# Steps of a mixer that runs between gather slots are moved one to five slots later

## The chip, the cores and the metric

The kernel runs on one core of a Trainium2 chip. The metric is the time of one launch in microseconds (us) on the device; the median of three runs is compared. A difference of under 0.2% (5 us) is not told from none here.

## What is computed

Two layers of a transformer-like backbone over 256 latent tokens `x` and 256 context tokens `ctx`, width 1024, float32. Cut to what matters:

```
for l in range(2):
    z = split(modulate(rms_norm(x), ...) @ w_in[l])          # 1968 columns, three mixers side by side
    mix = concat(pool_mixer(z), attention(z), mlstm(z)) @ w_out[l]
    x = x + g_a * mix                                        # context likewise, except in the last layer
    h = modulate(rms_norm(x), ...)
    q = (h @ peer_wq[l]); s = q . subkeys                    # 8 heads, two halves, 128 keys each
    experts = top 16 of the pair sums, per head              # 128 experts per token
    a = gelu(h . u_tab[expert]);  w = softmax(best) * a
    x = x + g_f * sum(w * v_tab[expert])
```

Each of the 128 tokens of a tile asks for 128 experts, each a row of 1024 `u` and 1024 `v` values (8 KB).

## The kernel before

**Slots.** The expert part runs over slots. In slot m, GpSimd (POOL) issues one gather of a row for each of 128 partitions, 1 MB together, into a free place (L772). VectorE (DVE) multiplies it with the token rows (`dot`, L1544). ScalarE (ACT) turns the sum into a coefficient and a diagonal matrix (`gated`, L1080, L1081, L1084: `gact`, `coef`, `diag`). TensorE (PE) adds the weighted `v` half (`values`, L1964); up to slot 336 of layer 0 it does two slots at a time, in the odd one. Then the place is free, and the next gather into it may be issued. Layer 0 has 512 slots (two context tiles, then two x tiles), layer 1 has 256.

**What runs between.** Mixer p stands for a layer and stream: p = 0 is the context's mixer of layer 0, before all slots and alone; p = 1, x's of layer 0, runs between slots 0 to about 200; p = 2, keys and values of the context in layer 1, from slot 268; p = 3 runs alone before layer 1's slots. Every engine's program is a generator that yields the slot number at which its next piece stands. `merge` puts the pieces in order, and `Behind.run(m)` gives out what is due after the engine's own work of slot m. So each engine has one fixed order, written out ahead; nothing is moved at run time, and a piece that waits holds up that engine's later slots.

**Places.** In slots 0 to 71 there are 7 places for gathered rows, then 8, from 134 on 9, and from 180 on more.

**Steps of p = 1 that the change touches** (slot of each in brackets):
- `norm1`: eight squares on ACT (L792; two each in 0 to 3), summed by PE (L1647; 2 to 5), `mean` on DVE (L1217; 6), `root` on ACT (L796; 7), `inverse` on DVE (L1221; 8), scaling on DVE and `modulate` on ACT.
- `projected`: ACT copies each of 16 groups of the input projection out of PSUM, three slots after PE begins it (L848 to L866).
- `gates`: ACT takes a logarithm (16, L873 to L875), DVE begins with it (17, L1252), PE turns the result (25), ACT copies it (26).
- `low_rank`: squares, `mean`, `root` and `inverse` of two further norms.
- the mLSTM, four heads, `ml` = 63, `ml_step` = 7. For head h, after 63 + 7h: PE makes scores (0, 1), DVE masks them (1, `masked`, L1334), ACT takes exponentials (2, `memory`, L928 and L931), DVE multiplies (4, 5, `weighted`, L1346), PE makes numerators (6, 7, L1764), ACT copies these (8, `numbers`, L939). `masked` of the next head waits for this head's numerators.

**Queries** for the experts are made between slots as well. PE forms query n in slots up to `ASKED[n]` (L1922), ACT copies it (`asked`, L1046), PE scores the keys two slots on (L1932), ACT copies these (`keys`, L1057, L1061), and DVE picks the best (L1472). One buffer `b_query` holds a query's sum: the next query's first part waits for `asked`. The weights of a query come into a ring of two (`qring`), loaded by SyncE (SP) once the scores of the query two before are done.

**SP** issues all weight loads in the one order of `ORDER`. `later` is four loads: the second part of `con`, layer 1's `par`, x itself and `poolw` (L748 to L751).

## Time and profile before

| what | value |
|---|---|
| median of three runs | 2608.3 us (2607.79 to 2610.45) |
| the profiled run | 2614.96 us |
| span of its trace | 2613.1 us |
| busy: PE, DVE, ACT, POOL | 2113.3, 1671.7, 1131.2, 819.3 us |
| moved by DMA | 940.07 MB, 805.36 MB of it by gathers |
| first gather issued, last row of PE's values in layer 1 begun | about 251 us, about 2601 us |

In a profile an instruction's own time is given beside the idle time of its engine before it, and behind an arrow what ended that idle time. Idle time alone costs nothing; it counts where the thing that is short (here mostly the DMA engines' time) is not used because of it.

### The profile page before, as it was taken

The numbers are of one execution on the slowest core, as the hardware profiler recorded it, in microseconds if no ns is written. First come the engines' busy times: TensorE is split into PE (matmuls) and PEld (weight loads), VectorE is DVE, ScalarE is ACT, GpSimd is POOL, SyncE is SP. The second block draws the span as 40 slices with busy tenths as digits, with TensorE's granted clock in tenths as the row PEclk, the third lists the DMA queues.
The fourth block names the chain that finished last, engine by engine and source line by source line (L and its number), as shares of the span: only waits on it lengthen the run. The fifth ranks groups of instructions, "written<-read, shape, count | busy, mean of one in ns | idle before, by whom it ended". The sixth has DMA issues, their size and how long they took to land.

```text
span 2613.1 us, 26759 instructions
## 1 busy us (share of the span) xinstructions
PE 2113.3 (81%) x8372; PEld 994.3 (38%) x8372; DVE 1671.7 (64%) x4135; ACT 1131.2 (43%) x3279; POOL 819.3 (31%) x772
## 2 busy tenths in 40 slices
PE   7988899776887777885777777699989987777776
PEld 4658555332443333441121111176874321211111
DVE  3484657678886766767667775335446666677654
ACT  3352544556663434644343333245333343433333
POOL 0000323343444334434434333100014443343331
PEclk8989999788999889997999999988899999999999
DMA  9783899999999999999999999811129999999997
GB/s 369 309 339 159 310 359 419 371 368 420 419 389 420 419 410 420 412 419 420 421 420 421 421 421 421 353 51 49 55 116 420 420 420 421 421 420 421 421 421 303
DMA packets 135885, 940.07 MB, mean 360 GB/s; under 512 B 14912, under 2 KB 18368, under 8 KB 25664
## 3 DMA queue, kind: packets, MB, share of 16 engines
q0 software_dynamic: 110592, 805.36, 75.0%
q1 hardware_dynamic: 23968, 131.70, 12.9%
q8 instruction: 66, 1.08, 0.2%
q10 hardware_dynamic: 1184, 1.32, 0.2%
q14 instruction: 75, 0.61, 0.1%
HBM read 937.27 MB, written 1.05 MB: 359 GB/s over the span
## 4 chain that ended last, share of the span: by engine, by line
DMA 45%; PE 36%; DVE 9%; ACT 7%; issue 2%; POOL 1%; SPq 1%; DVEq 0%; POOLq 0%; ACTq 0%
DMA mix<-uv_dram,idx 22%; DMA fast<-uv_dram,idx 19%; PE bank L1964 12%; PE bank L1922 5%; PE bank L1675 4%; DMA qring<-wq_dram 3%; DVE fast L1544 3%; PE bank L1880 2%; PE bank L1932 1%; PE bank L1669 1%; PE bank L1764 1%; DMA fast<-w_dram 1%; DVE mix L1544 1%; ACT diag L1084 1%; ACT coef L1081 1%
## 5 line engine op out<-in xcount | busy, mean ns | idle before, releaser
L1964 PE MATMUL bank<-fast,diag 128*64 128x512 f32 x2064 | 821.8, 658 | 257.4 <-ACT diag L1084 253.9
L772 POOL DMA_INDIRECT fast<-uv_dram,idx x516 | 559.8, 1085 | 1348.5 <-PE bank L1964 721.8
L1544 DVE SCALAR_TENSOR_TENSOR fast<-fast,hrow 128x1024 f32<-128x1024 f32 x516 | 630.4, 1223 | 358.9 <-DMA fast<-uv_dram,idx 354.0
L1080 ACT ACTIVATE gact<-araw 128x1 f32<-128x1 f32 x768 | 153.9, 200 | 855.2 <-DVE fast L1544 559.0
L1964 PEld LDWEIGHTS bank<-fast,diag 128*64 128x64 f32 x2064 | 198.2, 144 | 731.3 <-ACT diag L1084 469.9
L1964 PE MATMUL bank<-mix,diag 128*64 128x512 f32 x748 | 350.4, 622 | 100.2 <-ACT diag L1084 100.2
L1544 DVE SCALAR_TENSOR_TENSOR mix<-mix,hrow 128x1024 f32<-128x1024 f32 x187 | 229.0, 1226 | 151.7 <-DMA mix<-uv_dram,idx 151.6
L772 POOL DMA_INDIRECT mix<-uv_dram,idx x187 | 189.9, 1016 | 290.7 <-PE bank L1964 260.0
L1084 ACT ACTIVATE diag<-con,coef 128x64 f32<-128x64 f32 x768 | 267.1, 348 | 25.3
L1081 ACT ACTIVATE coef<-gact,wts 128x1 f32<-128x1 f32 x768 | 226.1, 294 | 25.0
L1964 PEld LDWEIGHTS bank<-mix,diag 128*64 128x64 f32 x748 | 84.6, 138 | 328.2 <-ACT diag L1084 219.4
L1922 PE MATMUL bank<-hT,qring 128*128 128x256 f32 x576 | 175.2, 420 | 34.1 <-DMA qring<-wq_dram 24.0
L1922 PEld LDWEIGHTS bank<-hT,qring 128*128 128x128 f32 x576 | 102.2, 197 | 140.8 <-issue 101.3
L1964 PE MATMUL bank<-hT,diag 128*64 128x512 f32 x204 | 101.8, 623 | 25.4 <-ACT diag L1084 25.3
L1544 DVE SCALAR_TENSOR_TENSOR hT<-hT,hrow 128x1024 f32<-128x1024 f32 x51 | 62.6, 1227 | 38.8 <-DMA hT<-uv_dram,idx 34.3
L1675 PE MATMUL bank<-hT,back 128*128 128x256 f32 (+1 forms) x336 | 83.7, 388 | 4.0 <-ACT hT L821 4.0
L1046 ACT ACTIVATE pq<-bank 128x256 f32<-128x256 f32 (+1 forms) x56 | 19.6, 350 | 134.7 <-PE bank L1922 134.5
L772 POOL DMA_INDIRECT hT<-uv_dram,idx x51 | 54.1, 1060 | 75.5 <-PE bank L1964 66.8
L1675 PE MATMUL bank<-hT,fast 128*128 128x256 f32 (+1 forms) x320 | 74.7, 389 | 1.3 <-ACT hT L821 1.3
L1675 PEld LDWEIGHTS bank<-hT,back 128*128 128x128 f32 (+1 forms) x336 | 63.8, 190 | 15.1 <-issue 4.4
L1080 ACT ACT_TABLE_LOAD x53 | 68.0, 1283 | 1.0
L1675 PEld LDWEIGHTS bank<-hT,fast 128*128 128x128 f32 (+1 forms) x320 | 60.2, 192 | 13.9 <-issue 5.4
(270 smaller groups left out, 2604.4 us busy)
## 6 DMA issues: line engine op xcount, KB each, us to landing
fast<-w_dram SPq DMA_DIRECT2D x72, 1024.0 KB, 8.3
qring<-wq_dram SPq DMA_DIRECT2D x36, 576.0 KB, 8.3
back<-w_dram SPq DMA_DIRECT2D x20, 1024.0 KB, 9.5
fast<-uv_dram,idx POOLq DMA_INDIRECT x516, 19.9
mix<-wq_dram SPq DMA_DIRECT2D x12, 576.0 KB, 10.4
mix<-uv_dram,idx POOLq DMA_INDIRECT x187, 23.9
fast<-uq_dram SPq DMA_DIRECT2D x4, 576.0 KB, 4.8
back<-uq_dram SPq DMA_DIRECT2D x2, 576.0 KB, 7.7
```

The costliest lines, as they stand in the source:

```text
L772: g.indirect_dma_start(slot(e, m), None, uv_tabs[e], bass.IndirectOffsetOnAxis(idx[:, Q % 2, n:n + 1], 0)).then_inc(landed[place], 16)
L1080: link(a.activation(gact[:, n:n + 1], araw[:, Q % 2, n:n + 1], ACT.Gelu))
L1081: link(a.activation(coef[:, n:n + 1], gact[:, n:n + 1], ACT.Copy, scale=wts[:, Q % 2, n:n + 1]))
L1084: a.activation(diag[:, m % DIAGS, :], two, ACT.Copy, scale=coef[:, n:n + 1]).then_inc(diag_ready.sem, 1)
L1544: v.scalar_tensor_tensor(out=u, in0=u, scalar=1.0, in1=hrow[:, (2 * i + half) % 3, :], op0=ALU.mult, op1=ALU.mult, accum_out=araw[:, Q % 2 ...
L1669: mm = t_.matmul(bank[g % 2][:, 0:WT], own_h(p)[:, k, n * P:(n + 1) * P], w[:, k, :], start=(k == 0), stop=(k == KC - 1))
L1675: mm = t_.matmul(bank[g % 2][0:rows, 0:SEQ], w[:, k, o:o + rows], own_h(p)[:, k, :], start=(k == 0), stop=(k == KC - 1))
L1764: mm = t_.matmul(memory_banks(p)[3][:, o:o + MD + 1], mE[:, e, kc, q * P:(q + 1) * P], v1[:, kc % 2, h, :], start=(kc == kcs[0]), stop=(kc ...
L1880: mm = t_.matmul(bank[b % 2][:, cs], w[:, k, b % 2 * P:b % 2 * P + P], own_h(p)[:, k, cs], start=(k == 0), stop=(k == KC - 1))
L1922: mm = t_.matmul(dst[:, cs], query_tile(e, u)[:, k, :], own_h(p)[:, k, cs], start=(k == 0), stop=(k == KC - 1))
L1932: mm = t_.matmul(b_aside[rows, j * P:(j + 1) * P], pq[:, n % 2, j * HALF:(j + 1) * HALF], query_tile(e, u)[:, KC, :], start=True, stop=True)
L1964: mm = t_.matmul(acc[half, f * 512:(f + 1) * 512], diag[:, j % DIAGS, :], slot(e, j)[:, D + f * 512:D + (f + 1) * 512], start=(j % SLOTS < ...
```

## The change

For p = 1, all but the attention, steps that wait for another engine are put one to five slots later (`lag`, and spelled out in `norm1`, which holds for p = 2 too). `asked` stands one slot later and `keys` two, in both layers. SP's `later` stands three weight loads later. No instruction is added or taken out. The core of the diff:

```diff
+def lag(p, slots_):
+    return slots_ if p == 1 else 0
...
-    order.append((-2000 + ADA_FIRST + 0.5, "later", 0))
+    order.append((-2000 + ADA_FIRST + 3.5, "later", 0))
...  # ACT, norm1
-                    yield k // 2 - early(p)
+                    yield k // 2 * (1 if alone(p) else 2) - early(p)
-                yield 7 - early(p)
+                yield 7 - early(p) + 2 * (not alone(p))
                 root(p, 1)
-                    yield 9 + (k + 1) // 3
+                    yield 9 + (k + 1) // 3 + (not alone(p))
...  # ACT, projected
-                    yield in_at(g) + 3
+                    yield in_at(g) + 3 + lag(p, 1)
...  # ACT, gates
-                yield GATE_AT + 3
+                yield GATE_AT + 3 + lag(p, 2)
-                    yield GATE_AT + 8
+                    yield GATE_AT + 8 + lag(p, 3)
-                yield GATE_AT + 11
+                yield GATE_AT + 11 + lag(p, 5)
...  # ACT, low_rank
-                yield at + 5
+                yield at + 5 + lag(p, 1)
-                            yield at + 3
+                            yield at + 3 + lag(p, 2)
-                    yield at + 7
+                    yield at + 7 + lag(p, 2)
...  # ACT, memory, then numbers
-                    yield at + 2
+                    yield at + 2 + lag(p, 1)
-                    yield TIMES[p].ml + TIMES[p].ml_step * h + TIMES[p].num + 2
+                    yield TIMES[p].ml + TIMES[p].ml_step * h + TIMES[p].num + 2 + lag(p, 2)
...  # ACT, experts
-                    if m in answer:
-                        asked(e, answer[m])
-                    if m - 2 in answer:
-                        keys(e, answer[m - 2])
+                    if m - 1 in answer:
+                        asked(e, answer[m - 1])
+                    if m - 4 in answer:
+                        keys(e, answer[m - 4])
...  # DVE, norm1 (mean, inverse, scaling)
-                yield 6 - early(p)
+                yield 6 - early(p) + 3 * (not alone(p))
-                yield 8 - early(p)
+                yield 8 - early(p) + 2 * (not alone(p))
-                    yield 8 + (k + 1) // 3 - early(p)
+                    yield 8 + (k + 1) // 3 - early(p) + 2 * (not alone(p))
...  # DVE, gates
-                at = GATE_AT + 2
+                at = GATE_AT + 2 + lag(p, 3)
...  # DVE, low_rank: mean and inverse, twice
-                yield at + 4
+                yield at + 4 + lag(p, 2)
-                yield at + 6
+                yield at + 6 + lag(p, 2)
-                    yield at + 6
+                    yield at + 6 + lag(p, 3)
-                    yield at + 8
+                    yield at + 8 + lag(p, 4)
...  # DVE, masked, weighted, combine
-                    yield TIMES[p].ml + TIMES[p].ml_step * h + 1
+                    yield TIMES[p].ml + TIMES[p].ml_step * h + 1 + lag(p, 2)
-                        yield TIMES[p].ml + TIMES[p].ml_step * h + 4 + e
+                        yield TIMES[p].ml + TIMES[p].ml_step * h + 4 + e + lag(p, 1)
-                yield at
+                yield at + lag(p, 2)
-                yield at + 1
+                yield at + 1 + lag(p, 1)
...  # PE, norm1, then gate_turns
-                    yield k // 2 + 2 - early(p)
+                    yield (k // 2 + 2 if alone(p) else k // 2 * 2 + 1) - early(p)
-                yield GATE_AT + 10
+                yield GATE_AT + 10 + lag(p, 3)
```

## Rows read from the trace of the kernel before

**Rows 1.** The page: busy times, and GB/s in 40 equal slices of the span.
```profile
PE 2113.3 (81%) x8372; PEld 994.3 (38%) x8372; DVE 1671.7 (64%) x4135; ACT 1131.2 (43%) x3279; POOL 819.3 (31%) x772
...
GB/s 369 309 339 159 310 359 419 371 368 420 419 389 420 419 410 420 412 419 420 421 420 421 421 421 421 353 51 49 55 116 420 420 420 421 421 420 421 421 421 303
```

**Rows 2.** Busy times by stretch: PE, PEld, DVE, ACT, POOL, then PEclk, DMA share, GB/s.
```profile
280.00:390.00 110.00, 98.73 (x458) 61.40 (x459) 68.50 (x168) 56.73 (x160) 34.94 (x32) 0.94 0.90 337
390.00:460.00 70.00, 64.38 (x287) 40.17 (x287) 51.48 (x128) 29.85 (x91) 23.53 (x23) 0.98 1.01 419
460.00:570.00 110.00, 83.72 (x353) 41.56 (x354) 75.07 (x186) 65.61 (x173) 45.01 (x38) 0.81 0.91 360
570.00:720.00 150.00, 111.61 (x504) 49.23 (x500) 133.16 (x351) 100.41 (x250) 66.81 (x57) 0.90 1.01 420
720.00:770.00 50.00, 40.08 (x206) 20.05 (x206) 38.95 (x104) 34.79 (x88) 22.45 (x19) 0.97 0.97 379
...
960.00:1060.00 100.00, 79.18 (x360) 35.86 (x360) 65.63 (x172) 42.99 (x145) 44.73 (x37) 0.91 1.00 410
```

**Rows 3.** Waits from 280 to 390 us: in total, times, longest.
```profile
ACT pq L1046 <- PE bank L1922: 16.9, 6, 4.8
...
DVE rms L1217 <- PE bank L1647: 12.9, 2, 6.7
PE bank L1964 <- ACT diag L1084: 12.7, 5, 4.4
...
DVE mix L1252 <- ACT mix L875: 8.8, 1, 8.8
```

**Rows 4.** Timeline of PE at slot 27: start, length, idle before.
```profile
372.48 0.70 PE L1922 MATMUL bank<-hT,qring 128*128 128x256 f32 x2 [1.69 <-DMA qring<-wq_dram]
```

**Rows 5.** The chain that ended last, at the same place: start, length.
```profile
361.31 11.13 DMA qring<-wq_dram
```

**Rows 6.** Waits from 460 to 570 us.
```profile
PE bank L1964 <- ACT diag L1084: 26.3, 6, 6.4
...
ACT mix L939 <- PE bank L1764: 10.7, 4, 4.4
DVE mix L1334 <- PE bank L1764: 10.3, 3, 4.8
```

**Rows 7.** Timeline of all engines around slots 71 to 73.
```profile
507.87 0.39 ACT L939 ACTIVATE mix<-bank 128x260 f32<-128x260 f32 x1 [4.38 <-PE bank L1764]
507.94 1.41 DVE L1334 TENSOR_TENSOR mix<-con,bank 128x256 f32<-128x256 f32 x4 [4.79 <-PE bank L1764]
509.27 1.22 DVE L1544 SCALAR_TENSOR_TENSOR qring<-qring,hrow 128x1024 f32<-128x1024 f32 x1
...
511.02 1.27 DVE L1544 SCALAR_TENSOR_TENSOR fast<-fast,hrow 128x1024 f32<-128x1024 f32 x1
511.46 1.28 ACT L928 ACT_TABLE_LOAD   x1
...
517.22 0.20 ACT L1080 ACTIVATE gact<-araw 128x1 f32<-128x1 f32 x1
518.18 1.11 PE L1964 MATMUL bank<-qring,diag 128*64 128x512 f32 x1 [6.36 <-ACT diag L1084]
```

**Rows 8.** Timeline of PE: the values of two slots, without and with idle time before.
```profile
489.42 1.94 PE L1964 MATMUL bank<-fast,diag 128*64 128x512 f32 x8
495.39 3.68 PE L1964 MATMUL bank<-fast,diag 128*64 128x512 f32 x8 [4.04 <-ACT diag L1084]
```

**Rows 9.** Timeline of PE in mixer 0, first expert-free stage.
```profile
39.85 1.94 PE L1610 MATMUL bank<-fast,hT 128*32 128x256 f32 x16 [4.68 <-DMA fast<-w_dram]
...
49.52 2.86 PE L1675 MATMUL bank<-hT,fast 128*128 128x256 f32 x12
```

**Rows 10.** Timeline of SP's queue: start, length of the issue.
```profile
18.13 0.43 SPq L748 DMA_DIRECT2D con<-con_dram  x1
...
19.81 10.72 SPq L751 DMA_DIRECT2D poolw<-pw_dram  x1
```

**Rows 11.** DMA issues: KB each, us to landing.
```profile
xT<-x_dram SPq DMA_DIRECT2D x1, 1024.0 KB, 18.1
...
con<-con_dram SPq DMA_DIRECT2D x1, 713.0 KB, 14.3
```

## The prediction

> **What bounds the kernel now.** I read the page first. The figure to see is GB/s in slices: 420 or 421 in most of both expert stages [rows 1]. There the DMA engines are full, and a slot costs what its megabyte costs: 1.05 MB / 421 GB/s = 2.49 us. Work of PE, DVE or ACT in such a slice is hidden by the queued gathers. The PE's 81% is an average that misleads: it says nothing of these slices.
>
> So I went by stretches and asked of each how much DMA time is unused, length x (1 - GB/s / 421) [rows 2]. From 280 to 390 us (slots 1 to 34): 110 x (1 - 337/421) = 21.9 us. From 460 to 570 us (slots 57 to 93, the mLSTM): 110 x (1 - 360/421) = 15.9 us. From 720 to 770 us (attention): 5.0 us. From 960 to 1060 us (where mixer 2 begins): 2.6 us. 390 to 460 and 570 to 720 us together: under 1 us. That is about 45 us, the most that any reordering between slots could give. Whatever the change does elsewhere is covered, as long as the places stay full.
>
> Then the waits of the two large stretches. In the first, PE is busy 98.7 of 110 us [rows 2]: PE itself is nearly the bound, so only its idle time can be won, 11.3 us. 12.7 us stand against `diag`, of which 4.4 are before slot 0 is valued [rows 3], not reached by the change: 8.3 us are. The engines behind those: DVE waits 12.9 us for the sums of squares and 8.8 us for the logarithm, ACT 16.9 us for queries [rows 3]. Each wait takes away the lead of DVE or ACT over PE, and PE pays when it comes to the next values. In the second, PE is idle 26.3 us of 110 and waits for `diag` in all of it [rows 2, 6].
>
> **Startup: `later` moves behind three weight loads.** PE waits 4.68 us for a weight tile, until 39.85 us [rows 9]. Ahead of that tile in SP's order stand `later`'s loads from 18.13 us on, and SP is held 10.72 us on their last [rows 10]. They are 1024 + 713 KB [rows 11] and, by the code, 261 KB of `par` and 64 KB of `poolw`: 2.1 MB, 5.0 us at 421 GB/s. So the tile lands near 34.8 us, about when PE began to wait (35.2). But the fourth tile after it still has the same bytes ahead of it: 39.8 + 3 x 2.49 = 47.3 us. It is the first that PE needs in its next projection group, at 49.52 us before [rows 9]. PE would be there at 44.8 and waits for it to 47.3. So of 4.68 us 2.5 come back as a wait, and 2.2 us are won; mixer 0 is then PE's own time. Bounds: 0 and 4.7. What is late next: x lands 7.5 us later, near 45 us, just before DVE's gates need it. I take -2.2.
>
> **Slots 0 to 34.** Squares go to every second slot, DVE's mean from slot 6 to 9, the gates from 17 to 20, the mean of the second norm from 25 to 27; each then stands behind the PE or ACT step it waits for, by one to four slots. The 12.9 and 8.8 us of DVE waits should go nearly whole, and DVE's dots run on. ACT's queries wait a slot less. Of the 8.3 us of PE idle I take 6: from slot 16 to 27 there is a second bound, the ring of query weights. Its load is issued when PE has scored the query two before, takes 11.13 us [rows 5], and PE already waits 1.69 us for it [rows 4]; three slots have to pass in that time, so a faster PE waits longer there. New costs: the gates' result comes three slots later, and nothing reads it before slot 50; ACT's pool copy and DVE's first use of it now stand in one slot (34), about 1 us on DVE, in a stretch with full DMA. Bounds: +6 (rival 3's query parts at half) and -11.3 (all PE idle). I take -6.
>
> **The mLSTM, slots 63 to 95.** One head in detail [rows 7]: DVE waits 4.79 us for the numerators of head 0, masks in 1.41 us, dots slot 72 at once and slot 73 at 511.02. ACT, also held by the numerators, makes `diag` of slot 72, then its burst of exponentials from 511.46 to 517.22 (5.8 us, two table loads in it), and only then `diag` 73. PE waits 6.36 us. The holds stand one behind the other: wait, mask, burst. After the change mask, burst and copy stand in slot 73. DVE and ACT do slots 72 and 73 first, in the time in which they waited, since those rows had landed: neither dot has idle time before it. PE then has two more slots of values ready, 1.94 us a pair when nothing idled before [rows 8], and the wait for numerators is over or short. The burst stays. Before: (10.3 + 10.7) us of waits for numerators in all [rows 6]; they overlap, so 10.3 once. Four heads: 26.3 us of idle less 10.3 less 4 x 1.94 = 8 us remain. New prices: ACT waits for the mask in its own slot, up to 1.4 us a head, 5.6 us on ACT; in slot 95 ACT waits for DVE's combine, about 2 us. In slot 87 the last head's exponentials follow the gates' softmax at once, which spares ACT one pair of table loads, 2 x 1.28 = 2.6 us [rows 7]. All that is PE idle time; the DMA time unused is 15.9 us and can't be won twice. With 18 of 26 us of the cause gone, less 5.6 for the mask, I take half and a bit: -9. Bounds: +6 (the mask's price alone) and -15.9.
>
> On the table loads the Trainium skill ("ScalarE: Activation LUTs", What ACT_TABLE_LOAD costs) puts a drain of about 1.38 us beside the 1.28 us, so the pair spared would be an estimated 5.3 us. The trace has no room for it: of the burst's 5.76 us two loads take 2.56, which leaves 0.40 us for each of its eight exponentials, and two drains more would leave 0.06; I go by 1.28.
>
> **The rest.** `asked` and `keys` later: from slot 203 on and in layer 1 DMA is full and places are many; `keys` stays ahead of the choice that reads it by two slots (slot 30 for 32, 62 for 64, 222 for 224). Mixer 2's norm: 2.6 us unused there; -0.5. Attention: untouched, 0. These are costed at nothing because of the gathers queued; were those stages not full, each `asked` would lay a query part (1.1 us) behind `diag` on PE.
>
> **Sum.** -2.2 - 6 - 9 - 0.5 = -17.7 us. The profiled run is 2614.96 us (span 2613.1), 6.7 over the median; the differences I take to be the same in both, so 2608.3 - 17.7 = 2590.6, say 2591.
>
> **Rivals.**
> 1. *Another engine's wait takes over* (DVE in the mLSTM, the query ring in slots 16 to 27). DVE is busy 75 of 110 us there [rows 2]; with the burst of 5.8 us still standing, each head may still miss the DMA by what it did less the wait. Then only a third is won: -2.2 - 2 - 4 = -8, 2600.
> 2. *All of it, and the clock.* After idle time the same eight matmuls take 3.68 us instead of 1.94 [rows 8], and from 460 to 570 us the granted clock is 0.81 [rows 2], so PE is at its lower level (1.2 of 2.4 GHz) some 38% of the time. If the idle gaps close, PE also gets faster, and the mLSTM stretch fills the DMA: -4 - 9 - 15.9 = -29, 2579. The Trainium skill ("TensorE: Matmul & The Clock Gate", HAM oscillation) prices such idling at half of the throttled time, here an estimated 21 us of PE time; by it this rival would be the forecast.
> 3. *No lead to spend* (slower). The later steps help only if DVE and ACT can pass PE by two slots, which needs landed rows. With 7 or 8 places, a row lands only after PE frees its place; if the rows aren't there, every wait stays and the prices come on top: 5.6 for masks, 2 for combine, and for queries 8 to 15 a part of 1.1 to 2.05 us laid behind `diag` on PE, 12.5 us in all. At half of that, with startup's 2.2 gone as well: +10, 2618. It decides where a dot after a stall has idle time for a landing. Against it: the dots of slots 72 and 73 had none [rows 7].
> 4. *Nothing measurable*: gains of slots 0 to 34 eaten by the query ring, the mLSTM's by the burst: 2606.
>
> **How the numbers follow.** Forecast (-12 to -23) 0.48; rival 1 0.20; rival 2 0.13; rival 4 0.11; rival 3 0.08. The predicted time is the forecast's. Faster by over 0.2% is the forecast and rivals 1 and 2, 0.81; within 0.2% 0.11; slower 0.08. The range leaves out rival 3 and the outer parts of 2 and 4: 2576 to 2607. The forecast's own range is 2585 to 2596.
>
> **What would show it.** Right: GB/s of the fifth and sixth slice (261 to 392 us) up from 310 and 359, of the eighth and ninth from 371 and 368 towards 420; DVE's waits at L1217 and L1252 of p = 1 under 2 us; PE's first rest tile near 35 us without idle time, and a new wait of some 2.5 us at the next group; granted clock in the mLSTM over 0.85; first gather issued about 2 us sooner. Wrong: ACT idle before L928 of over 2 us a head (the masks' price), dots waiting for DMA landings before slot 95, or longer waits for `qring`.

## The result, and the profile after

The changed kernel takes 2593.7 us (2587.5 to 2597.9 in six runs; a seventh was disturbed and doesn't count) beside 2610.45 us (2606.1 to 2615.3 in seven) for the kernel before. The ratio is 0.9929, with a 95% interval from 0.9915 to 0.9943: 0.0071 x 2610 = 18.5 us less (the two medians alone lie 16.8 us apart). The forecast was 17.7 us less. Below, "worth so many us" is always such a ratio less one, times the median of before, taken against runs of the kernel before that went along with the experiment. The intervals reach some 2 to 4 us to either side, so the difference of two such worths is uncertain by about 5 us.

The two profiled executions lie apart by more than that: the span is 2585.5 us after and 2613.1 before, 27.6 us, because the one fell at the low end of its runs and the other at the high end. A stage's length from one profile therefore has to be held against other profiles before it is believed, and I do that with the experiments.

Line numbers move with the edits: a line of the kernel before stands six lines later in the kernel after, and ten or more later in the experiments, so ACT's `asked` is L1046, L1052 and L1056 in turn.

The page of the kernel after, busy times and GB/s in 40 slices, to be read against [rows 1]:

```profile
PE 2100.6 (81%) x8372; PEld 990.6 (38%) x8372; DVE 1672.4 (65%) x4135; ACT 1136.6 (44%) x3279; POOL 829.9 (32%) x772
...
GB/s 390 302 354 144 361 393 418 403 401 420 415 402 420 419 410 410 409 420 420 421 421 421 421 421 421 304 67 34 56 162 420 420 420 421 421 421 421 421 421 303
```

The work is the same to the instruction. What differs most while the slots of layer 0 run is the fifth, sixth, eighth and ninth slice: 361, 393, 403 and 401 GB/s where there was 310, 359, 371 and 368. By stretch, columns as in [rows 2]; the first line is slots 1 to 34, the third the mLSTM, and the second and fourth are the same slots cut as tightly as the experiments' below. The last two lines are the kernel before, cut in the same way:

```profile
270.00:380.00 110.00, 101.39 (x485) 63.72 (x486) 76.63 (x193) 66.13 (x181) 38.06 (x33) 0.97 0.95 379
273.00:377.00 104.00, 97.33 (x464) 61.27 (x466) 73.82 (x184) 63.27 (x173) 37.12 (x32) 0.97 0.95 377
450.00:560.00 110.00, 84.17 (x349) 39.09 (x346) 86.65 (x212) 67.29 (x180) 46.74 (x42) 0.83 0.99 399
443.00:550.00 107.00, 84.23 (x362) 41.10 (x362) 80.35 (x191) 66.52 (x179) 46.03 (x41) 0.85 0.99 399
...
278.00:394.00 116.00, 102.73 (x475) 63.51 (x476) 73.27 (x182) 59.83 (x171) 36.03 (x33) 0.94 0.91 342
459.00:575.00 116.00, 86.96 (x366) 42.97 (x364) 80.58 (x192) 68.28 (x180) 49.16 (x42) 0.82 0.92 364
```

Unused DMA time, reckoned as in the prediction: 110 x (1 - 379/421) = 11.0 us where 21.9 stood, and 110 x (1 - 399/421) = 5.7 us where 15.9 stood. PE is busy 101.4 of 110 us in the first (98.7 before), and its clock in the second went from 0.81 to 0.83. Cut tightly, the first stretch is 12 us shorter, with PE busy 97.33 us where it was 102.73, at a clock of 0.97 where it was 0.94.

The waits of the first stretch (273 to 377 us), against [rows 3]:

```profile
DVE fast L1550 <- DMA fast<-uv_dram,idx: 28.1, 16, 3.8
...
ACT pq L1052 <- PE bank L1928: 11.3, 7, 2.4
...
PE bank L1653 <- ACT mix L798: 3.3, 1, 3.3
PE bank L1928 <- DMA qring<-wq_dram: 2.8, 2, 2.3
```

PE's 12.7 us for `diag` are gone altogether, also the 4.4 us that the prediction took to be out of reach (3.3 us for a square of the first norm, L1653, stand there now). Gone too are DVE's 12.9 us for the sums and 8.8 us for the logarithm. DVE now waits for landing rows instead: 28.1 us. In the trace of a kernel whose end is set by the gathers that is the good sign, DVE has caught up with the DMA.

The waits of the mLSTM (443 to 550 us), against [rows 6]:

```profile
PE bank L1970 <- ACT diag L1090: 22.2, 7, 8.4
DVE fast L1550 <- DMA fast<-uv_dram,idx: 20.5, 15, 2.5
...
DVE mix L1340 <- issue: 3.5, 1, 3.5
ACT mix L934 <- DVE mix L1340: 3.0, 2, 2.4
...
ACT L934 <- DVE mix L1340: 1.3, 1, 1.3
```

ACT's 10.7 us for the numerators are gone. Of DVE's 10.3 us 3.9 remain: 0.44 us at head 1, and the 3.5 us that the view puts down to "issue". Those are the mask of head 3, which waits for head 2's numerators; it starts when these end, at 526.17 + 1.78 = 527.95 us:

```profile
526.17 1.78 PE L1770 MATMUL bank<-mix 128*128 128x65 f32 x14
...
528.05 1.42 DVE L1340 TENSOR_TENSOR mix<-con,bank 128x256 f32<-128x256 f32 x4 [3.47 <-issue]
```

PE's wait for `diag` has hardly fallen: 22.2 us remain of 26.3. The place of [rows 7] after, one head around slots 72 and 73 (start, length, idle time before):

```profile
488.96 1.28 ACT L934 ACT_TABLE_LOAD   x1
...
489.31 1.42 DVE L1340 TENSOR_TENSOR mix<-con,bank 128x256 f32<-128x256 f32 x4 [0.44 <-PE bank L1770]
...
490.64 1.22 DVE L1550 SCALAR_TENSOR_TENSOR fast<-fast,hrow 128x1024 f32<-128x1024 f32 x1
490.76 0.91 ACT L934 ACTIVATE mix<-mix,gcol 128x256 f32<-128x256 f32 x2 [0.52 <-DVE mix L1340]
...
497.26 1.94 PE L1970 MATMUL bank<-fast,diag 128*64 128x512 f32 x8 [0.53 <-ACT diag L1090]
```

Mask and burst now come behind the `diag` of slot 73; the mask waits 0.44 us instead of 4.79, ACT waits 0.52 us for the mask, and the dot behind the mask starts with no idle time for a landing. PE's wait behind the burst is 0.53 us instead of 6.36. The other heads are less fortunate. PE's two longest waits, at heads 0 and 2, then ACT's burst ahead of the first of them, and then the same burst in the kernel before:

```profile
478.68 3.68 PE L1970 MATMUL bank<-fast,diag 128*64 128x512 f32 x8 [8.37 <-ACT diag L1090]
...
515.42 1.11 PE L1970 MATMUL bank<-qring,diag 128*64 128x512 f32 x1 [4.45 <-ACT diag L1090]
```

```profile
471.84 1.28 ACT L934 ACT_TABLE_LOAD   x1 [1.31 <-DVE mix L1340]
...
476.43 1.28 ACT L1086 ACT_TABLE_LOAD   x1
```

```profile
487.88 1.28 ACT L928 ACT_TABLE_LOAD   x1
```

Head 0 has no numerators before it, so there was nothing to win, and ACT now waits 1.31 us for the mask ahead of its burst of 471.84 to 477.71 us. PE's last values begin at 468.37 and end at 470.31, 1.5 us ahead of the burst, so PE stands through all of it, 8.37 us. Before, PE had work until 491.36 us [rows 8], 3.5 us into the burst that begins at 487.88. Head by head PE waits 8.37, 0.53, 4.45 and 2.21 us behind the burst; before it was 4.04 [rows 8], 6.36 [rows 7], 3.84 and 6.36.

Startup, PE and SP's queue, against [rows 9, 10]:

```profile
36.57 1.94 PE L1616 MATMUL bank<-fast,hT 128*32 128x256 f32 x16
...
47.33 5.01 PE L1681 MATMUL bank<-hT,fast 128*128 128x256 f32 x22 [1.23 <-DMA fast<-w_dram]
```

```profile
27.98 10.42 SPq L757 DMA_DIRECT2D poolw<-pw_dram  x1
```

PE is at that group at 47.33 us, where it was at 49.52.

### The profile page after: what moved, and what is told of

Same layout as the page of the kernel before. It is cut to its first block, busy times and chain, and to the rows that moved or that the text cites. A ratio compares the mean times of both kernels' runs of the same rounds, so it can differ in the third digit from the quotient of the medians.

```text
span 2585.5 us, 26758 instructions
## 1 busy us (share of the span) xinstructions
PE 2100.6 (81%) x8372; PEld 990.6 (38%) x8372; DVE 1672.4 (65%) x4135; ACT 1136.6 (44%) x3279; POOL 829.9 (32%) x772
## 4 chain that ended last, share of the span: by engine, by line
DMA 46%; PE 36%; DVE 8%; ACT 6%; issue 3%; POOL 1%; SPq 1%; another core or an unknown queue 0%; DVEq 0%; POOLq 0%; ACTq 0%
DMA mix<-uv_dram,idx 22%; DMA fast<-uv_dram,idx 20%; PE bank L1970 12%; PE bank L1928 5%; PE bank L1681 5%; PE bank L1886 3%; DMA qring<-wq_dram 3%; DVE fast L1550 2%; PE bank L1675 2%; PE bank L1938 1%; DVE mix L1550 1%; PE bank L1653 1%; PE bank L1770 1%; PE bank L1869 1%; ACT diag L1090 1%
## 5 line engine op out<-in xcount | busy, mean ns | idle before, releaser
L1970 PE MATMUL bank<-fast,diag 128*64 128x512 f32 x2064 | 810.2, 648 | 235.3 <-ACT diag L1090 229.4
L778 POOL DMA_INDIRECT fast<-uv_dram,idx x516 | 566.3, 1097 | 1312.9 <-PE bank L1970 687.2
L1090 ACT ACTIVATE diag<-con,coef 128x64 f32<-128x64 f32 x768 | 267.1, 348 | 25.2
L1928 PEld LDWEIGHTS bank<-hT,qring 128*128 128x128 f32 x576 | 102.5, 198 | 148.2 <-issue 111.2
L1886 PE MATMUL bank<-hT,fast 128*128 128x128 f32 x512 | 62.4, 277 | 0.8 <-DVE hT L1440 0.8
```

What stands on the lines that cost most here:

```text
L778: g.indirect_dma_start(slot(e, m), None, uv_tabs[e], bass.IndirectOffsetOnAxis(idx[:, Q % 2, n:n + 1], 0)).then_inc(landed[place], 16)
L1090: a.activation(diag[:, m % DIAGS, :], two, ACT.Copy, scale=coef[:, n:n + 1]).then_inc(diag_ready.sem, 1)
L1886: mm = t_.matmul(bank[b % 2][:, cs], w[:, k, b % 2 * P:b % 2 * P + P], own_h(p)[:, k, cs], start=(k == 0), stop=(k == KC - 1))
L1928: mm = t_.matmul(dst[:, cs], query_tile(e, u)[:, k, :], own_h(p)[:, k, cs], start=(k == 0), stop=(k == KC - 1))
L1970: mm = t_.matmul(acc[half, f * 512:(f + 1) * 512], diag[:, j % DIAGS, :], slot(e, j)[:, D + f * 512:D + (f + 1) * 512], start=(j % SLOTS < ...
```

## The experiments

Each undoes or keeps a part of the change. Since one profile of a stage says little by itself, I counted in every trace when DVE starts its dot of slots 1, 35, 57 and 96 and when the first gather is issued, and in slots 57 to 96 also PE's idle time and its granted clock. I call `asked` and `keys` the asks. In us, the last column the time by the ratio:

```
                            first    slots    slots  PE idle    PEclk   against
                           gather     1-35    57-96    57-96    57-96    before
before (profiled first)     251.2    116.0    115.7     28.6     0.82
only later's loads          246.8    114.3    116.5     25.2     0.78      -1.0
only the front              251.6    114.3    109.0     31.5     0.87      -3.6
only the mLSTM              252.2    115.1    107.4     19.3     0.79      -6.3
asks, norm1                 249.2    104.6    109.9     28.3     0.86      -6.8
asks, front                 252.3    108.4    112.2     26.4     0.82      -8.6
all but the asks            247.7    114.9    106.2     23.4     0.84     -13.3
before, once more           252.4    115.6    110.2     27.4     0.83      +0.8
asked and norm1             252.5    105.9    111.7     28.0     0.85      -1.6
asked and norm1, again      251.1    108.2    116.9     28.7     0.82      -1.6
after (the change)          246.2    104.1    106.9     22.8     0.85     -18.5
exponentials left out       248.7    104.5    101.5     17.1     0.88     -21.4
burst in two slots          249.2    102.5    114.5     27.0     0.81      -7.6
burst in two, two waits     246.3    104.8    113.5     21.6     0.80     -10.9
```

The column of slots 57 to 96 scatters from 109.0 to 116.9 us in the eight traces without the mLSTM's lags (before twice, only later's loads, only the front, and the four with asks but no mLSTM), though these slots are the same there but for the asks. PE's idle time doesn't follow: it is 25.2 to 31.5 us, largest in the shortest stretch. PE's busy time does, from 77.4 us at a clock of 0.87 to 91.4 at 0.78. So much of this scatter goes with the granted clock; whether the clock is its cause or follows it, these traces don't say. In the mean the eight have 112.8 us with 28.0 idle, and the three with the lags and the whole burst in one slot (only the mLSTM, all but the asks, after) 106.8 us with 21.8 idle: the 6.0 us are PE's idle time, and its busy time is the same (84.8 and 85.0).

### Startup alone

```diff
 # against the kernel before
-    order.append((-2000 + ADA_FIRST + 0.5, "later", 0))
+    order.append((-2000 + ADA_FIRST + 3.5, "later", 0))
```

> The kernel before with SP's later loads alone moved behind three weight loads. Theory A (the prediction's: PE's wait of 4.68 us goes, 2.5 us of it come back at the next projection group, all else is unchanged): first gather 2.2 us sooner than before, total -2.2 us, within 0.2%. Theory B (mixer 0 gains more than the wait, as the first gather of the changed kernel, 5.0 us sooner, would say): first gather and total -4 to -5 us.

Measured: ratio 0.9996 (0.9985 to 1.0008), 1.0 us less. The first gather went out at 246.8 us instead of 251.2. In six traces with the loads moved the first gather is issued between 246.2 and 249.2 us, in eight without between 249.2 and 252.5; the means are 247.5 and 251.6. So the loads do move the first gather, by about 4 us where the forecast said 2.2, but the time shows 1.0 us, and by the interval 4 us at the most. Where in mixer 0 the second 2 us are won wasn't traced.

### The front alone

Kept: the lags of the first norm, the projections' copies, the gates and the low-rank norms. Back to before: `later`, the mLSTM, `asked` and `keys`.

```diff
 # against the kernel after: later and the mLSTM back to before, and
-                    if m - 1 in answer:
-                        asked(e, answer[m - 1])
-                    if m - 4 in answer:
-                        keys(e, answer[m - 4])
+                    if m in answer:
+                        asked(e, answer[m])
+                    if m - 2 in answer:
+                        keys(e, answer[m - 2])
```

> The kernel before with only the lags of norm1, projected, gates and low_rank (slots 0 to 60). Theory A (each part wins its own stretch): dot of slot 35 about 8 to 11 us sooner, measured from the first gather; total -8 to -11 us. Theory B (the later queries are what freed slots 0 to 34, the lags need them): dot 35 at most 4 us sooner, total -4 us or less.

Measured: 0.9986 (0.9975 to 0.9997), 3.6 us less. But slots 1 to 35 take 114.3 us, no less than the 114.3 to 116.0 of the traces without any lag there. This was the surprise. The waits from 279 to 394 us:

```profile
ACT pq L1056 <- PE bank L1932: 24.2, 8, 4.7
...
PE bank L1974 <- ACT diag L1094: 7.6, 2, 3.8
```

DVE's waits for the sums and the logarithm are gone, as forecast (another, 7.5 us for ACT's root, is as long as before), and ACT's wait for queries grew from 16.9 to 24.2 us. The timeline of PE and ACT shows how that holds a slot (same kernel, slots with local queries):

```profile
293.29 1.94 PE L1974 MATMUL bank<-fast,diag 128*64 128x512 f32 x8
...
295.59 2.05 PE L1932 MATMUL bank<-hT,mix 128*128 128x128 f32 x16
...
297.68 0.28 ACT L1056 ACTIVATE pq<-bank 128x128 f32<-128x128 f32 x1 [2.39 <-PE bank L1932]
...
298.44 1.94 PE L1974 MATMUL bank<-fast,diag 128*64 128x512 f32 x8
```

PE computes a query part (2.05 us), ACT stands idle 2.39 us to copy it and only then goes on, and the values are 298.44 - 293.29 = 5.15 us apart. The same place in the kernel after, with the copy a slot later:

```profile
292.62 1.94 PE L1970 MATMUL bank<-fast,diag 128*64 128x512 f32 x8
...
294.92 2.05 PE L1928 MATMUL bank<-hT,mix 128*128 128x128 f32 x16
...
296.90 1.94 PE L1970 MATMUL bank<-fast,diag 128*64 128x512 f32 x8
...
297.73 0.26 ACT L1052 ACTIVATE pq<-bank 128x128 f32<-128x128 f32 x1
```

No wait, and the values are 4.28 us apart.

### The mLSTM alone

```diff
 # against the kernel before: only these, for p = 1
-                    yield at + 2
+                    yield at + 2 + lag(p, 1)
...
-                    yield TIMES[p].ml + TIMES[p].ml_step * h + TIMES[p].num + 2
+                    yield TIMES[p].ml + TIMES[p].ml_step * h + TIMES[p].num + 2 + lag(p, 2)
...
-                    yield TIMES[p].ml + TIMES[p].ml_step * h + 1
+                    yield TIMES[p].ml + TIMES[p].ml_step * h + 1 + lag(p, 2)
...
-                        yield TIMES[p].ml + TIMES[p].ml_step * h + 4 + e
+                        yield TIMES[p].ml + TIMES[p].ml_step * h + 4 + e + lag(p, 1)
...
```

> The kernel before with only the mLSTM's lags (masked, memory, weighted, numbers, combine). Theory A: slots 57 to 96 take 9 us less, all else as before, total -9 us. Theory B (no lead to spend: rows have not landed, waits stay): under 3 us less, ACT waits over 2 us before each burst of exponentials.

Measured: 0.9976 (0.9965 to 0.9988), 6.3 us less, the largest single part. Slots 57 to 96 take 107.4 us, at 390 GB/s, and that at a granted clock of 0.79, lower than in either profile of the kernel before. PE still waits for `diag` there:

```profile
461.00:568.00 107.00, 87.70 (x352) 44.63 (x350) 80.16 (x191) 63.82 (x174) 41.86 (x38) 0.79 0.98 390
```

```profile
PE bank L1974 <- ACT diag L1094: 19.3, 5, 7.8
```

### The queries, with and without the rest of the front

I first wrote a kernel with the queries' lag alone, but that one would never end: by the code, where mixer 2 starts with the first norm unspread, PE's sum stands behind a query part that waits for ACT's copy, and ACT's copy behind the square that waits for PE's sum. So the smallest kernel with this lag has the spread of the first norm too.

```diff
 # against the kernel after: later and the mLSTM back, and every other lag at nothing
 def lag(p, slots_):
-    return slots_ if p == 1 else 0
+    return 0
```

> The kernel before with asked and keys later and norm1 of p = 1 and 2 spread, no other lag, later not moved. Theory B (the queries held ACT and so PE in slots 0 to 34): the stretch from the first gather to the dot of slot 35 is 7 to 11 us shorter than the 142 us of before, total -5 to -8 us. Theory A (the prediction's: queries later are worth nothing): stretch at most 3 us shorter, total within 3 us.

Measured: 0.9974 (0.9962 to 0.9986), 6.8 us less, and slots 1 to 35 in 104.6 us. The windows and the waits from 276 to 381 us:

```profile
276.00:381.00 105.00, 98.11 (x475) 61.92 (x476) 74.01 (x185) 60.84 (x171) 36.17 (x33) 0.98 0.96 377
```

```profile
DVE rms L1227 <- PE bank L1657: 6.5, 1, 6.5
ACT pq L1056 <- PE bank L1932: 6.1, 5, 1.9
...
DVE mix L1262 <- ACT mix L885: 4.0, 1, 4.0
```

DVE still waits 10.5 us of the 21.7 that the forecast wanted gone, and the stretch is as short as after. So it wasn't DVE's waits that held these slots. Part of what is won here is the clock: in the six traces without asks PE is idle 11.1 to 13.7 us and busy 100.8 to 103.2 in slots 1 to 35, at a granted clock of 0.94; in the eight with asks it is idle 5.6 to 9.8 us and busy 96.7 to 99.8, at 0.95 to 0.98. In the means 5.3 us of idle time and 4.3 us of busy time are gone.

With all of the front and the asks (`later` and the mLSTM back to before):

> The kernel before with asked and keys later and all lags of slots 0 to 60, without the mLSTM's and without moving later. Theory B: stretch to the dot of slot 35 10 to 12 us shorter, total -9 to -11 us, more than the queries with norm1 and the front lags alone (3.6 us) together would make if the two need one another. Theory A: as the front lags alone, -4 us.

Measured: 0.9967 (0.9954 to 0.9981), 8.6 us less. Beside the front alone the asks are worth 8.6 - 3.6 = 5.0 us; beside asks and norm1 the other lags of the front are worth 8.6 - 6.8 = 1.8 us, which is not told from nothing.

### The change without the asks

```diff
 # against the kernel after
-                    if m - 1 in answer:
-                        asked(e, answer[m - 1])
-                    if m - 4 in answer:
-                        keys(e, answer[m - 4])
+                    if m in answer:
+                        asked(e, answer[m])
+                    if m - 2 in answer:
+                        keys(e, answer[m - 2])
```

> The changed kernel with asked and keys back at their old slots. Theory B: 6 to 8 us of the 18.5 are lost, all of them before slot 35: total -11 us, the sum of the parts alone (1.0 + 3.6 + 6.3). Theory A: 0 to 2 us lost, total -17 to -18 us.

Measured: 0.9949 (0.9935 to 0.9963), 13.3 us less, with slots 1 to 35 in 114.9 us. The asks are worth 18.5 - 13.3 = 5.2 us here and 5.0 above: nearly the same figure twice, each uncertain by about 5 us. From 275 to 390 us:

```profile
ACT pq L1056 <- PE bank L1932: 30.7, 9, 5.3
...
PE bank L1974 <- ACT diag L1094: 7.6, 2, 3.8
```

The kernel before went along as well, unchanged, for a second profile of it:

> The kernel before, unchanged, for a second profile: what two executions of one program differ by, stage by stage. Both theories: total 0 within 2 us. If the first profile of before was an average one, first gather at 251 us and slots 57 to 96 in 116 us again; if it was a slow one in that stage, as the profiles of the front lags alone and of the mLSTM's lags alone suggest (109 and 107 us), about 109 us.

Measured: 1.0003 (0.9993 to 1.0014). Slots 57 to 96 take 110.2 us in it and 115.7 in the first profile; slots 1 to 35 take 115.6 and 116.0. So the first stretch repeats well, and the second doesn't. The second here:

```profile
462.00:572.00 110.00, 82.89 (x350) 39.39 (x346) 80.39 (x191) 66.21 (x174) 49.51 (x40) 0.83 0.94 374
```

### Only `asked`, with the keys as before

```diff
 # against "asks, norm1" above
-                    if m - 4 in answer:
-                        keys(e, answer[m - 4])
+                    if m - 2 in answer:
+                        keys(e, answer[m - 2])
```

> As the run with asked, keys and norm1, but keys at their old slots (two after the query): only ACT's copy of the query is a slot later. Theory C (it is ACT's wait for the query, 16.9 us in slots 1 to 34, that held PE): slots 1 to 35 take 104 to 107 us, total about -6.8 us as with both. Theory D (it is the wait for the scores, through keys): 112 to 115 us, total within 3 us.

> The kernel with only asked a slot later (and norm1 spread) once more, since its stretch from slot 1 to 35 was 10 us shorter in the profile and its time only 1.6 us. If the time was an unlucky set: ratio 0.997 to 0.998, as with keys. If the profile's gain is given back in executions that aren't profiled: 0.999 again, and the stretch in the profile about 105 us.

Measured: 0.9994 (0.9985 to 1.0003), and in the second run of it 0.9994 (0.9984 to 1.0003): 1.6 us less both times. Slots 1 to 35 take 105.9 and 108.2 us, 7 to 10 us less than without, and yet the time hardly moves. With the keys moved as well it is 6.8 us less. The 1.6 us have intervals of -0.8 to 3.9 and 4.2 us, the 6.8 us one of 3.7 to 9.9, so the difference is likely real, but not by much. What takes the gain of the first stretch away again in these two I haven't settled; see below.

### What is left of the burst

Here the exponentials of x's mLSTM in layer 0 are left out, with plain copies in the place of half of them and a maximum for the subtraction in DVE's mask, so the output differs; the question is what ACT's burst still costs after the change.

```diff
 # against the kernel after, for p = 1 only
-                        for j in range(2):
+                        for j in range(0 if p == 1 else 2):
                             ins = a.activation(mE[:, e, j, :], mE[:, e, j, :], ACT.Exp, ...)
+                        if p == 1:
+                            for j in (2, 3):
+                                ins = a.activation(mE[:, e, j, :], ..., ACT.Copy, scale=-1.0)
```

> The changed kernel, leaving out x's exponentials in the mLSTM of layer 0: of eight with two table loads per head (5.8 us of ACT) four plain copies stay (about 1.7 us), and the mask is a maximum, so that the numbers stay finite. Theory E (the burst is what still idles PE 22 us in slots 57 to 96): PE's waits for diag there fall under 10 us, the unused DMA time of 5 to 6 us goes, total 4 to 6 us under the changed kernel, 0.991 of before falls to 0.990 or less. Theory F (PE and DMA are full enough already; the idle time is hidden): PE idles less, time within 2 us of the changed kernel's.

Measured: 0.9918 (0.9904 to 0.9932), 21.4 us less, 2.9 us under the change; by the two intervals that is not told from nothing, and the stretch is the better witness. The windows of the mLSTM:

```profile
446.00:547.00 101.00, 83.93 (x364) 39.89 (x364) 79.90 (x191) 51.07 (x156) 45.94 (x41) 0.88 1.01 419
```

Now the DMA engines are as busy as in the full slices (419 GB/s) and the stretch is 5.4 us shorter. PE still waits 14.9 us for `diag`, with no DMA time left for it to cost.

### Spreading the burst

```diff
 # against the kernel after: ACT, memory
                     for e in range(DIRS):
+                        if p == 1 and e:
+                            yield at + 3 + lag(p, 1)
```

> The changed kernel with the burst of exponentials of a head in two slots, one direction in each, for two table loads more per head. Theory E: each hold of ACT is 3.5 instead of 5.8 us plus the wait for the mask; PE idles a few us less, total 1 to 3 us under the changed kernel. Theory F: no difference; if ACT's longer work (10 us in all) counts, up to 3 us over it.

Measured: 0.9971 (0.9960 to 0.9982), 7.6 us less than before, 10.9 us more than the change. The slots take 114.5 us, and DVE waits, from 445 to 559 us:

```profile
PE bank L1976 <- ACT diag L1096: 24.1, 8, 8.7
...
DVE mix L1358 <- ACT mix L943: 15.8, 4, 4.6
```

DVE's weights of the first direction waited for both halves. The next kernel lets them go after the first (a semaphore of its own for it), to tell that wait from the table loads that a split adds:

```diff
 # against the split
+                        if p == 1 and e == 0:
+                            ins.then_inc(mE_half, 1)
...
-                        v.wait_ge(mE_ready.sem, mE_ready.at(p, h + 1))
+                        if p == 1 and e == 0:
+                            v.wait_ge(mE_half, h + 1)
+                        else:
+                            v.wait_ge(mE_ready.sem, mE_ready.at(p, h + 1))
```

> As the split burst, but DVE's product of the first direction waits only for that direction's exponentials. Theory G (the split lost because DVE waited 15.8 us for the second half): that wait falls under 6 us, slots 57 to 96 take 104 to 108 us again, total between the changed kernel's ratio 0.993 and 0.992. Theory H (the two table loads more per head, 10 us of ACT work, are what it lost): the stretch stays over 111 us, ratio 0.995 or more.

Measured: 0.9958 (0.9946 to 0.9970), 10.9 us less than before and still 7.6 more than the change. From 441 to 555 us:

```profile
441.00:555.00 114.00, 92.66 (x378) 47.31 (x374) 79.98 (x192) 78.75 (x190) 46.62 (x40) 0.81 0.94 376
```

```profile
491.93 0.91 ACT L941 ACTIVATE mix<-mix,gcol 128x256 f32<-128x256 f32 x2
...
493.87 1.28 ACT L1095 ACT_TABLE_LOAD   x1
...
496.09 1.28 ACT L941 ACT_TABLE_LOAD   x1
...
499.03 1.28 ACT L1095 ACT_TABLE_LOAD   x1
```

DVE's wait fell from 15.8 to 3.6 us, and 3.3 of the 10.9 us came back (within the noise of the two), with the stretch at 113.5 us. So the larger part isn't that wait. The rows show two loads more a head; 8 x 1.28 = 10.2 us of the 12.2 by which ACT is busier (78.75 and 66.52 us, in windows of 114 and 107 us) are theirs. But waits between mask and numerators also came back in this kernel (ACT 5.4 us for the mask, DVE 5.0 for the numerators), so that the 7.6 us are the loads' is not shown. The table speaks for another reading as well: PE's idle time is 21.6 us here and 22.8 in the kernel after, and what is longer is PE's busy time (92.66 and 84.23 us), at a clock of 0.80 or 0.81 instead of 0.85. With one profile of each that stays open. None of the kernels that do all the work beats the change.

## Why the prediction was right, and where it wasn't

**The sum.** Forecast and measured are 0.8 us apart (-17.7 and -18.5). That closeness is in good part luck: the measured interval alone reaches 3.7 us to either side, and the terms are off in both directions. -2.2, -6 and -9 were measured, part by part, as -1.0, -8.8 (-3.6 and -5.2) and -6.3, each with some 3 us or more to either side.

**What bounds the kernel.** Right. The four slices named moved by 32 to 51 GB/s; of the others between the fifth and the 25th only the twelfth and the sixteenth moved by 10 or more (389 to 402, 420 to 410). Unused DMA time fell by 10.9 and 10.2 us in the two stretches. It also bounded the gain: with the burst away the stretch runs at 419 GB/s and leaves nothing more to win there.

**Startup, -2.2.** The mechanism is right: PE takes its rest tiles at 36.57 us with no idle time (4.68 before), and the next group waits for its tile until 47.33 us, by the forecast 47.3. Of the new wait of 2.5 us only 1.23 show, because PE got there later than the 44.8 us reckoned: its group before ended at 46.10. The first gather then goes out 4 us sooner in the means, not 2.2. By itself the move is worth 1.0 us with an interval of 3 us either way, in which 2.2 lies; this term is neither borne out nor refuted in time.

**Slots 0 to 34, -6.** The size is near, the reason is wrong. The step that failed is "The 12.9 and 8.8 us of DVE waits should go nearly whole, and DVE's dots run on", taken as what frees PE, and with it "These are costed at nothing" for `asked` and `keys` in **The rest**. DVE's waits did go, but without the asks slots 1 to 35 take 114.3 to 116.0 us in six traces, whether the front's lags are there or not; with the asks they take 102.5 to 108.4 us in eight, also where half of DVE's waits stay. ACT's wait for queries is what holds these slots, and DVE's waits had lain beside it: with them gone the other only grows, 16.9 us, then 24.2 and 30.7. A smaller step failed too, "PE itself is nearly the bound, so only its idle time can be won": of the 9.7 us by which the stretch is shorter with asks, 4.3 are PE's busy time at the higher clock. Where the 3.6 us of the front alone come from, if not from here, no stretch shows above its scatter. The prediction had the row of 16.9 us in hand and gave it a sentence without a price. That was rival 1's mechanism, another engine's wait takes over, with a place that it hadn't named.

**How much of that counts.** The asks take some 10 us from slots 1 to 35 in the traces and 5.0 and 5.2 us from the time. Where the difference goes shows in part: slots 236 to 280 take 120.4 us in the mean of the six traces without asks and 122.1 in the eight with, 1.7 us given back. In layer 1 the stretch from its first gather to slot 540 gains 2.7 us (95.4 to 92.7), which the one behind it, with full DMA, takes back in full (574.1 to 576.8). That leaves about 3 us, no more than the uncertainty of the 5 us. It doesn't lie in slots 57 to 96, where the four traces with asks and the four without, all without the mLSTM's lags, have the same mean (112.7 and 112.9 us). For the runs with `asked` alone more than 3 us is missing. Why `keys` makes the difference between 1.6 and 6.8 us stays open too.

**The mLSTM, -9.** The mechanism is right and the size probably too large: alone it is worth 6.3 us, with an interval that just reaches 9 (3.1 to 9.1), and in the means of the traces 6.0 us (112.8 and 106.8), all of it idle time of PE. The step that failed is "With 18 of 26 us of the cause gone": PE's wait for `diag` went from 26.3 to 22.2 us, not to 8. Of the 10.3 us for numerators 6.4 went; DVE's 3.5 us at head 3 are the same wait again. The head that I had worked out in detail came as forecast (0.53 us), and I took it four times. At head 0 the wait grew from 4.04 to 8.37 us: it had no numerators to win, the mask's price of 1.31 us came on top, and PE had run out of work 1.5 us before the burst began. At head 2 it stayed (3.84 and 4.45). ACT waited 4.3 us for masks in all, with 5.6 reckoned, but 2.4 of them are head 3's, where the mask itself was late. The pair of table loads that was to be spared in slot 87 was: ACT comes to head 3's exponentials without a load of its own. And 15.9 us of unused DMA time was the figure of one execution at the long end: the second profile of the same kernel has 110 x (1 - 374/421) = 12.3 us there.

**The rest and mixer 2, -0.5.** The parts measured alone come to -1.0 - 3.6 - 6.3 = -10.9 us, the change without asks to -13.3; with intervals of 3 to 4 us to either side of each these agree. Mixer 2's own term is too small to be seen. The asks then bring -18.5.

**The rivals.** Rival 1 happened to parts of the change, not to the whole. Rival 2, all idle gaps closed and the clock with them, happened to a part of slots 1 to 35, where the clock rose with the asks (0.94 to 0.97 in the two profiles). In the mLSTM it did not: some 22 of 28 us of PE's idle time stayed, and the 0.85 of the kernel after (0.82 before, tightly cut) lies inside the 0.78 to 0.87 of the traces without the lags, so no rise is shown. The prediction had wanted it over 0.85. Neither did the half of the throttled time by the Trainium skill ("TensorE: Matmul & The Clock Gate", HAM oscillation), an estimated 21 us, come back: 6.3 us did. As the clock stayed low, this doesn't test the page's price. With the burst away the clock is 0.88, and the stretch falls by no more than the DMA had left. Rival 3, no lead to spend, is refuted at its own place: the dot behind the mask had no idle time for a landing, and DVE waited 0.44 us. The prediction also had dots waiting for landings before slot 95 among its signs of being wrong. They did wait, 20.5 us in 15 waits (13.3 in 8 before), and the time fell all the same: near full DMA that sign says nothing. `qring` stayed a small bound: 2.8 us in two waits, and 2.7 in two before.

## What to carry to other kernels

Before moving the steps of one wait, list every wait between the same engines in that stretch, and price each as if the others were gone: here a row of 16.9 us, passed over, was worth some 5 us, and the two of 12.9 and 8.8 us that the argument rested on came with 3.6. When the transfers are the bound, reckon the time in which they are unused, by stage and from at least two executions: it caps the gain, and it scattered by 4 us between two profiles of one kernel. Split a stage's length into an engine's busy and idle time before you compare two profiles: here the scatter was in the busy time, at a lower clock, and the gain in the idle time. And in this kernel the burst was better moved behind work that is ready than cut in two, where each piece has its own table loads.

## What the runs showed of the hardware

Cutting ACT's exponentials into two visits added two table loads of 1.28 us a head, and the next activation began 0.01 to 0.02 us after each (495.43 + 1.28, next at 496.73 in the split kernel). A small load whose place in SP's order is right behind x's 1024 KB held the queue for 10.42 us wherever the group was put (10.72 before). And PE's clock in the mLSTM did not simply follow PE's waits: it was 0.79 with a wait of 19.3 us for `diag` (only the mLSTM), 0.85 with 22.2 (after), 0.82 with 26.3 (before) and 0.88 with 14.9 (exponentials left out). Over slots 1 to 35 it did rise where those waits were gone: 0.94 in the two profiles of before with 12.7 us, 0.98 with none (asks, norm1).
